# A hybrid decoder layer with a mixture of experts: combines moved behind the gather, transposes and down products reordered, staging copies cut in halves, and the loads reordered

## The reference, cut to what matters

```python
logits = x2 @ w_router + b_router
top_vals, top_idx = lax.top_k(logits, 4)          # 4 of 32 experts
gates = softmax(top_vals)
# for each expert e and the tokens that chose it:
gu = xb @ w_up[e] + b_up[e]                       # w_up[e]: 1024 x 2048
gate, up = gu[:, :1024], gu[:, 1024:]
gate = minimum(gate, 7); up = clip(up, -7, 7)
act = (up + 1.0) * (gate * sigmoid(1.702 * gate))
out = act @ w_down[e] + b_down[e]                 # w_down[e]: 1024 x 1024
y[token] += out * gates
```

## Time and profile before

| | |
|---|---|
| median of 3 runs | 1309.75 us (1308.13 to 1313.57) |
| profiled execution | 1305.46 us, its span 1303.7 us |
| PE busy | 1170.0 us, 90% of the span |
| DVE busy | 659.5 us, 51% |
| GpSimd busy | 549.4 us, 42% |
| ACT busy | 248.6 us, 19% |
| moved by DMA | 448.97 MB, mean 344 GB/s |

### The profile page before, as it was taken

How to read it: one execution, slowest core, us unless ns; L and a number is a source line. 1 busy time by engine, 2 the same in 40 slices (tenths; PEclk the granted TensorE clock), 3 DMA queues, 4 the chain that set the end, 5 groups by cost and what they waited for, 6 DMA issues and landing times.

```text
span 1303.7 us, 29658 instructions
## 1 busy us (share of the span) xinstructions
PE 1170.0 (90%) x11113; PEld 576.9 (44%) x11114; DVE 659.5 (51%) x1161; ACT 248.6 (19%) x483; POOL 549.4 (42%) x368
## 2 busy tenths in 40 slices
PE   8999999999889988889897888998988978988986
PEld 7777777766333333333332333333333323333332
DVE  2999983123665436426441664264353435435444
ACT  2012123001122211222121212221221212212212
POOL 0012300000554645637470555374474645555671
PEclk9999999999899989999998999998999989999998
DMA  8983334652988999999998799999999999999995
GB/s 258 344 266 126 129 130 164 260 197 85 381 354 352 397 422 385 415 422 405 424 421 355 289 365 414 422 403 423 416 395 423 422 422 417 406 422 408 404 422 212
DMA packets 94570, 448.97 MB, mean 344 GB/s; under 512 B 8526, under 2 KB 42894, under 8 KB 45339
## 3 DMA queue, kind: packets, MB, share of 16 engines
q1 hardware_dynamic: 93742, 446.55, 86.1%
q10 hardware_dynamic: 749, 1.19, 0.3%
q0 software_dynamic: 48, 0.85, 0.2%
HBM read 447.00 MB, written 2.42 MB: 345 GB/s over the span
## 4 chain that ended last, share of the span: by engine, by line
PE 54%; DVE 24%; DMA 16%; issue 3%; DVEq 2%; ACT 1%; POOL 0%; SPq 0%; ACTq 0%; POOLq 0%
PE banks L1379 19%; DMA ring<-in_w_down 16%; PE banks L1389 10%; DVE arena L802 8%; PE banks L1177 7%; PE banks L1092 5%; PE banks L1129 4%; DVE WT L760 3%; DVE banks L1033 2%; PE banks L1293 2%; PE banks L1136 2%; PE banks L1157 2%; DVE WT L770 2%; DVE WT L762 1%; DVE hT L1035 1%
## 5 line engine op out<-in xcount | busy, mean ns | idle before, releaser
L535 POOL COPY ring<-arena 128x2048 f32<-128x2048 f32 x279 | 518.6, 1917 | 553.7 <-PE banks L1379 378.5
L1379 PE MATMUL banks<-ring,hT 128*32 128x512 f32 x3328 | 423.5, 605 | 28.1 <-DVE hT L778 28.1
L1389 PE MATMUL banks<-ring,hT 128*32 128x256 f32 x3328 | 227.0, 392 | 51.4 <-DMA ring<-in_w_down 51.4
L1033 DVE TENSOR_TENSOR banks<-banks,bupT 128x512 f32<-128x512 f32 x52 | 36.4, 700 | 416.9 <-PE banks L1092 416.9
L1389 PEld LDWEIGHTS banks<-ring,hT 128*32 128x32 f32 x3328 | 103.2, 112 | 194.2 <-issue 83.5
L1177 PE MATMUL banks<-hT,ring 128*128 128x288 f32 x768 | 188.4, 406 | 0.3 <-ACT hT L558 0.3
L770 DVE TENSOR_SCALAR WT<-slot_ids,prod 128x128 f32 x153 | 139.7, 969 | 87.8 <-PE banks L1092 87.8
L1379 PEld LDWEIGHTS banks<-ring,hT 128*32 128x32 f32 x3328 | 99.2, 111 | 171.6 <-issue 137.8
L1177 PEld LDWEIGHTS banks<-hT,ring 128*128 128x128 f32 x768 | 145.1, 190 | 39.7 <-issue 0.4
L802 DVE SCALAR_TENSOR_TENSOR arena<-arena 128x256 f32<-128x256 f32 x240 | 108.1, 529 | 0.0
L760 DVE TENSOR_SCALAR WT<-slot_ids,prod,ss 128x32 f32 x104 | 106.2, 1065 | 0.7 <-issue 0.7
(11 more groups left out here) (248 smaller groups left out, 715.0 us busy)
## 6 DMA issues: line engine op xcount, KB each, us to landing
arena<-in_w_up SPq DMA_DIRECT2D x248, 1024.0 KB, 12.3
ring<-in_w_down SPq DMA_DIRECT2D x97, 1024.0 KB, 10.9
arena<-in_w_down SPq DMA_DIRECT2D x31, 1024.0 KB, 13.9
ring<-in_w_in SPq DMA_DIRECT2D x24, 1024.0 KB, 10.8
ring<-in_w_up SPq DMA_DIRECT2D x8, 1024.0 KB, 4.8
ring<-in_w_branch_b SPq DMA_DIRECT2D x4, 1024.0 KB, 5.0
ring<-in_w_branch_a SPq DMA_DIRECT2D x4, 1024.0 KB, 5.0
ring<-in_w_out SPq DMA_DIRECT2D x4, 1024.0 KB, 5.0
```

The source lines that it names most:

```text
L535: nc.gpsimd.tensor_copy(ring[:, k, :], parked[k]).then_inc(slot_full[k], 16)
L1033: V.tensor_tensor(turned, turned, bias.unsqueeze(2).to_broadcast([P, 16, BLK]), ALU.add).then_inc(biased, 1)
L1379: ins = mm(UP[g * BLK:(g + 1) * BLK, :], xT[:, k, :], ring[:, k, g * 512:(g + 1) * 512], start=k == 0, stop=k == UP_SLOTS - 1)
L1389: ins = mm(DN[q * BLK:(q + 1) * BLK, 0:256], actT[:, f % 4, f // 4, :], ring[:, UP_SLOTS + j, h * D + q * 256:h * D + (q + 1) * 256], star ...
```

## The change

Seven edits in one step:

- PE: in each body both prompt combines and the sample combine come right behind the gather, after a wait for `combT_ready` and `out_ready`; before, the first one (tt=0) lay between up slots 6 and 7, and before the loop.
- PE: `turn_rows` comes ahead of `turn_raw`.
- PE: the down slots lie behind up slots 3 to 6 instead of 1 to 4, and `turn_weights` with them.
- DVE: `add_before` and `take_x` come first in the body; `select` comes ahead of `select_weighted`.
- GpSimd: each staging copy of 2048 columns is two of 1024, the second waiting for the first; a semaphore `slot_free` is added.
- SP: the direct loads of slots 9 to 11 come behind three staged loads instead of eight.
- ACT raises `out_ready` once before the loop, when the bias rows of `w_down` are in.

```diff
+BEHIND = 3
...
             def next_weights(place, here, after, before):
 
-                load_parked_again(place + 1, after, range(UP_SLOTS))
+                load_parked_again(place + 1, after, range(BEHIND))
                 load_direct(here, before, range(PARKED, SLOTS))
-                load_parked_again(place + 1, after, range(UP_SLOTS, PARKED))
+                load_parked_again(place + 1, after, range(BEHIND, PARKED))
...
+                    pool.sem_inc(slot_free, 1)
+                    pool.wait_ge(slot_free, (e - 1) * PARKED + k + 1)
                     pool.wait_ge(parked_full[k], 16 * e)
-                    nc.gpsimd.tensor_copy(ring[:, k, :], parked[k]).then_inc(slot_full[k], 16)
+                    nc.gpsimd.tensor_copy(ring[:, k, 0:D], parked[k][:, 0:D]).then_inc(half_copied, 1)
+                    pool.wait_ge(half_copied, (e - 1) * PARKED + k + 1)
+                    nc.gpsimd.tensor_copy(ring[:, k, D:SLOT], parked[k][:, D:SLOT]).then_inc(slot_full[k], 16)
...
             nc.scalar.copy(combT, TB[:, 0:T]).then_inc(combT_ready, 1)
+            act.wait_ge(bdown_in, 16 * QN)
+            act.sem_inc(out_ready, 1)
...
             with dve.Fori(0, bodies) as i:
...
+                add_before(i)
+                take_x(i + 1)
                 activate(i, column)
-                take_x(i + 1)
                 swish(i)
-                add_before(i)
+                dve.wait_ge(gathered, i + 2)
+                select(column2)
                 dve.wait_ge(combT_turned, i + 1)
                 select_weighted(column1)
-                dve.wait_ge(gathered, i + 2)
-                select(column2)
+            add_before(bodies)
...
             def combine_before(i, stop):
 
-                combine(1, total[1], False, stop)
+                pe.wait_ge(combT_ready, i + 1)
+                pe.wait_ge(out_ready, i + 1)
+                for tt in range(2):
+                    combine(tt, total[tt], False, stop and tt == 1)
                 combine_sample(DN[:, 256:512]).then_inc(combined, 1)
...
-            pe.wait_ge(bdown_in, 16 * QN)
-            pe.wait_ge(combT_ready, 1)
-            combine(0, total[0], False, False)
...
                 gather()
+                combine_before(i, False)
+                turn_rows(i + 1)
                 turn_raw(i)
-                turn_rows(i + 1)
-                combine_before(i, False)
                 pe.wait_ge(xT_ready, i + 2)
                 for k in range(UP_SLOTS):
                     up(k, after)
-                    if k == 1:
+                    if k == BEHIND:
                         turn_weights(i)
                         pe.wait_ge(y_added, i + 1)
-                    if 1 <= k <= DOWN_SLOTS:
-                        down(k - 1, here)
-                    if k == 6:
-                        pe.wait_ge(combT_ready, i + 2)
-                        pe.wait_ge(out_ready, i + 1)
-                        combine(0, total[0], False, False)
+                    if BEHIND <= k < BEHIND + DOWN_SLOTS:
+                        down(k - BEHIND, here)
...
+            combine_before(bodies, True)
             turn_raw(bodies)
-            combine_before(bodies, True)
```

More of the change, by code:

```diff
@@ L227, in hybrid_layer @@
         old_rows_stored = sem("old_rows_stored")
+        half_copied, slot_free = sem("half_copied"), sem("slot_free")
         up_used, down_used = sem("up_used"), sem("down_used")
@@ L1054, in _ @@
                     dve.value_load(items[0:1, bass.ds(i + n, 1)], min_val=0, max_val=COLUMN_MAX) for n in range(3))
+                add_before(i)
+                take_x(i + 1)
                 activate(i, column)
-                take_x(i + 1)
                 swish(i)
-                add_before(i)
+                dve.wait_ge(gathered, i + 2)
+                select(column2)
                 dve.wait_ge(combT_turned, i + 1)
                 select_weighted(column1)
-                dve.wait_ge(gathered, i + 2)
-                select(column2)
+            add_before(bodies)
             activate(bodies, dve.value_load(items[0:1, bass.ds(bodies, 1)], min_val=0, max_val=COLUMN_MAX))
             swish(bodies)
-            add_before(bodies)
             for tt in range(2):
@@ L1465, in _ @@
             pe.wait_ge(combT_ready, bodies + 2)
-            pe.wait_ge(out_ready, bodies + 1)
+            pe.wait_ge(out_ready, bodies + 2)
             pe.wait_ge(total_added, 2)
```

## The result

The changed kernel takes 1288.26 us (median of 4 runs, 1287.87 to 1291.3), the kernel before 1308.94 beside it (1306.19 to 1313.57): a ratio of 0.9844, with a 95% interval of 0.9811 to 0.9876. It is some 20 us faster; the forecast was 1303.7, with a range of 1292 to 1318, so the result lies outside it. The profiled execution has a span of 1286.4 us where before had 1303.7.

The account below looks back on a forecast made before the run. The load queue was taken as the bound over all, 914 us plus 53 lost, with PE close. Loss terms +5, -5, -8 and +1 gave -7, taken as -6: 1299.5 us profiled, 1303.7 as median, range 1292 to 1318.

Parts of the forecast that it names:

- The steady part: 409 to 710 and 760 to 1270 us: queue loss, 18.0 us before, was to change by -5 us (0 to -12).
- slower rival: The hold empties the queue at each two-item place, up to 9 us a time: +10, 1319.5 us; chance 0.20.
- The body: One pass of PE's loop, gather to gather, was to go from 16.53 to 16.25 us.
- The step from the profiled execution to the median: The median was taken 4.3 us above the profiled execution, as before: 1299.5 becomes 1303.7 us.
- Up to 409: Start of the stage: queue loss, 14.6 us before, was to change by +5 us (0 to +9).
- The hold: Six staged loads wait for `down_used`: queue empty 14 us in the stage's first body, no cost in steady state.
- 700 to 760: Around the place of three items, predicted as 710 to 760: queue loss, 18.2 us before, to change by -8 (-3 to -12).
- End: PE's tail after the last landing, 5.3 us before, was to change by +1 us (-3 to +2).
- Halved copies: GpSimd staging: 1.05 us a half copy, 2.4 a slot; DVE operations held 1.0 us instead of 1.9.
- Stands: PE waits at copied up slots, some eleven of 6 to 12 us, in place of those for direct down blocks.
- The clock rival: PE stays at 1.2 GHz over a series of up slots: +5, 1315 us; counted within the slower rival's 0.20.
- the gains come through: Starting hold half as long and a deeper queue at 418 of 422 GB/s: median 1295 us; chance 0.22.

Follow-up runs that it names:

- c4: The kernel before with `select` ahead of `select_weighted` alone; 1296.30 us, ratio 0.9864.
- e1: The changed kernel with the old order of loads and the sample combine issued three times in each body; 1288.87 us, ratio 0.9835.
- c1: The kernel before with both prompt combines behind the gather, right before the sample combine, none between up slots 6 and 7; 1294.19 us, ratio 0.9856.
- a4: The changed kernel with SP's old order of loads; 1278.58 us, ratio 0.9750.
- f1: The changed kernel with the old order of loads for the first six places of SP's loop; 1278.72 us, ratio 0.9732.
- a1: The kernel before with SP's new order of loads alone; 1303.31 us, ratio 0.9932.

## Why the prediction was wrong

- *The steady part, -5 (0 to -12)*: this is the step that failed, measured at -15.5; it makes 10.5 of the 10.6 us by which the ledger's steps, -17.6 in all, miss the forecast's -7 (the others miss by +3.2, -4.1 and +0.8). It rested on "the lost gather waits come back as longer stands", and, in the part on bounds, on an edit being worth "what it takes from those 53 us, not what it takes from PE". That the stage ends with its last load holds, and the ledger closes. That what is taken from PE is worth nothing doesn't follow: the 18 us of the steady part were lost where PE was the bound, so work or waits taken from PE are taken from them. c4 and e1 show it from both sides: in c4, of the gather's 22.4 us only 6.4 came back as stands for down blocks (57.8 against 51.4). The rows to see it in were in the trace: not stretches of 300 us, where both engines look nearly full, but those of 5 to 10 us with PE at 100% and the queue under its rate. The prediction had 33.1 against 29.8 us for a two-item place, and used it only for its slower rival.
- *The body, 16.25*: it is 15.59. From gather to first up the prediction had 4.7; it is 4.34, because PE had waited 0.57 us for `take_x` there, and the third combine fits into that wait (0.22 is left). The combine between slots 6 and 7 was priced at its own 0.64; without it the way from first up to gather is 11.25 instead of 12.18, so it was worth 0.93. (In c1, where it alone goes, that way is 11.03, and the combine was worth 1.15: 0.64 of its own, 0.11 ahead of it, and 0.39 between the start of slot 7 and the gather, 0.18 of them idle. Whether its shape or its wait for `out_ready` costs the rest, no run separates.) Together -0.94 a body instead of -0.28, 48 us of PE over 51 bodies.
- *The step from the profiled execution to the median*: the forecast kept the 4.3 us by which the median of before lay above its profiled execution. The changed kernel's lies 0.1 above, so 4.2 of the 15.4 us between 1303.7 and 1288.26 are of this kind, and no term of the ledger has them.
- *Up to 409, +5 (0 to +9)*: +0.9 net, but in parts it held. The order costs an empty piece of 8.3 us (14 was forecast) and 10.2 us of this stretch against a4. The stretch's old loss shrinks with the new loop and the halves, 14.6 to 5.3 in a4; the prediction had only 2 us for that, and the first gather of the loop, at 345.19 before, comes at 340.52 in the changed kernel, 4.7 us earlier.
- *The hold*: SP's issues in the changed kernel (start, length, count), against the earlier trace rows:

```profile
333.36 4.72 SPq L405 DMA_DIRECT2D arena<-in_w_up  x3
351.99 3.76 SPq L401 DMA_DIRECT2D ring<-in_w_down  x3
355.93 3.29 SPq L405 DMA_DIRECT2D arena<-in_w_up  x5
```

  Place and mechanism are as forecast; the next issue comes at 351.99, not 354.5, and the third staged block lands at 344.6, not 341.5. "In steady state the hold costs nothing" is borne out by f1.
- *700 to 760, -8 (-3 to -12)*: -4.8, within its bounds. Cut at 685 it is 18.3 before, 15.8 in a4, 13.3 with the order: half of it is the order's, as argued, and half comes with the loop and the halves.
- *End, +1*: +1.8.
- *Halved copies*: 1.05 us a half, as taken; two in 2.21 us (547.12 to 549.33 in GpSimd's timeline) where 2.4 was taken for a slot. `select_weighted` went from 969 to 690 ns on the mean, and the gather's waits are gone, as forecast.
- *Stands*: eleven of over 2 us at copied slots, as forecast, nine of 8.24 to 8.88 us and two shorter than the 6 to 12 foreseen (4.06 and 4.95).
- *The count of places*: twelve of one item, nineteen of two and one of three make 53 items, and there are 52. The first place has one item, for GpSimd refills its slots from 329.7 us on, before the loop: thirteen, eighteen and one. The sum doesn't use it.
- *The range* of 1292 to 1318 leaves out the 1319.5 of the prediction's own slower rival.
- *The clock rival* foresaw PE slow over a whole series of slots. One stand in PE's timeline of the changed kernel:

```profile
519.58 1.93 PE L1387 MATMUL banks<-ring,hT 128*32 128x512 f32 x8 [8.79 <-POOL ring L541]
521.44 0.93 PE L1100 MATMUL banks<-ident,WT 128*128 128x128 f32 x3
522.30 1.38 PE L1397 MATMUL banks<-ring,hT 128*32 128x256 f32 x16
523.51 1.03 PE L1387 MATMUL banks<-ring,hT 128*32 128x512 f32 x8
```

  A slot takes 1.93 us right behind the stand, at the lower level of 1.2 GHz (granted clock 0.50 in 519.60 to 521.40), and 1.03 from 3.9 us on (granted clock 1.00 in 523.50 to 526). There is no series: the wait comes once, the slots after it follow without one, and the granted clock of 409 to 700 is 0.95 against 0.96 before. The Trainium skill (TensorE: Matmul & The Clock Gate, the part on HAM oscillation) has bursts between DMA waits running cold each time; the first slot behind this stand agrees with its 1.93 us, and so do those behind nine of the other ten (1.59 to 1.94), but that is once a stand and not once a block.
- *The rival "the gains come through"* had the right sign and 1295 us. Its reason, that PE stands at each one-item expert and so every block counts that comes earlier, isn't the one found: these stands grew from 51 to 94 us while the time fell, and what was won is backlog that the places of two items no longer drain.
- *The slower rival*, a queue emptied by the hold at each two-item place, is refuted for the changed kernel by f1 and by its single empty piece at the start. On the slow loop of a1, where the backlog was gone again at three later places, it is partly true.

## What to carry to other kernels

A kernel can be bound by its queue over all and by an engine at some places: cut the saturated stretch finely, and look for slices where the engine is at 100% and the queue is under its rate, before calling that engine's waits free; then look what the engine did ahead of each late landing. Count what each kind of iteration asks of either side (35.3 against 29.8 us here), since a backlog that drains in a run of one kind is paid for though the mean has room. When loads are reordered behind a wait, see what is in the queue at the first iteration, where no backlog covers it.

## What the runs showed of the hardware

A block of 1 MiB landed 2.49 us behind the one before with three or more loads outstanding, and in a4 with two as well (2.50; in the kernel before, where one of two mostly came behind a late one, 2.75). It landed 3.24 us behind it on the mean of the 17 loads of the kernel before that were the only one. Four of these had been issued less than 1 us before the landing ahead of them, and took 3.45 to 4.14 us; no first packet of a load comes sooner than 0.95 us behind its issue. But thirteen had been issued 6.9 to 10.2 us before, and still took 2.52 to 3.88, 3.05 on the mean. So this queue lost some of its 422 GB/s before it was empty. Why isn't shown. More than three outstanding gave nothing more.

A combine of 0.64 us between up slots 6 and 7 cost PE 1.15 us in all (c1) or 0.93 (the changed kernel).

Two copies of 1024 columns on GpSimd are 2.10 us of work where one of 2048 is 1.92, 0.18 us more; by their closest pace, a pair every 2.15 us (344.00 and 346.15 in the changed kernel's timeline) against eight whole copies in 14.77, it is 0.30. The Trainium skill (GPSIMD Engine Reference, section 3.1) has a fixed cost for each GpSimd instruction; the 0.18 us agree with there being one, and it is small beside the halves' gain on the kernel before.
